# Two transformer blocks on one core: three DVE low halves, one small product, the expert loads and a gather put at other places

## The reference

```python
h = h + g1[:, None, :] * ((ga * y_ret + gb * y_dsa) @ w_o[l])
u2 = modulate(rmsnorm(h, norm_ffn_g[l]), sh2, sc2)
h = h + g2[:, None, :] * hier_moe(u2, ...)
...
gl = (t @ w_gr + b_gr)                  # 4 groups: each token takes its best group
gsel = jnp.argmax(gl, axis=-1)
el_sel = ...                            # the 4 experts of that group
vals, ids = lax.top_k(el_sel, 2)        # two experts of it, with softmax weights
hid = silu(x @ w1[e]) * (x @ w3[e]) * gate
y = sum over e of hid @ w2[e]
```

## Time and profile before

| what | value |
|---|---|
| median of 3 runs | 750.55 us (749.89 to 751.17) |
| the profiled execution | 748.99 us |
| its span, first to last instruction | 747.7 us |
| PE busy | 713.5 us (95%) |
| DVE busy | 500.1 us (67%) |
| ACT busy | 379.3 us (51%) |
| POOL busy | 90.6 us (12%) |
| HBM read | 162.33 MB, mean 219 GB/s |
| mean granted TensorE clock | 0.998 |

### The profile page before, as it was taken

One profiled execution on the slowest core, in us unless ns is written; L12 is line 12 of the kernel. 1 busy time (PEld: TensorE's weight loads), 2 busy tenths in 40 slices (PEclk: granted clock), 3 DMA queues, 4 the chain that ended last, 5 costly groups with the idle time before them and its releaser, 6 DMA issues.

```text
span 747.7 us, 9899 instructions
## 1 busy us (share of the span) xinstructions
PE 713.5 (95%) x3766; PEld 573.2 (77%) x3766; DVE 500.1 (67%) x738; ACT 379.3 (51%) x549; POOL 90.6 (12%) x71
## 2 busy tenths in 40 slices
PE   3899999999999989899999999989999999999997
PEld 0587766778788867788887777769888877788886
DVE  1464784345578773765577898887998675565854
ACT  1354423556445333743557786757634538644532
POOL 0252484330010000000000000011001500000000
PEclk9999999999999999999999999999999999999999
DMA  9999886757336940656678999964444575545541
GB/s 318 362 289 375 279 322 238 253 201 258 107 138 206 357 140 10 192 197 194 187 231 294 368 355 358 366 231 141 144 139 140 149 222 164 158 127 196 169 140 57
DMA packets 100670, 164.07 MB, mean 219 GB/s; under 512 B 10768, under 2 KB 45293, under 8 KB 100494
## 3 DMA queue, kind: packets, MB, share of 16 engines
q1 hardware_dynamic: 98718, 155.53, 62.6%
q0 software_dynamic: 1904, 7.90, 3.1%
HBM read 162.33 MB, written 1.08 MB: 219 GB/s over the span
## 4 chain that ended last, share of the span: by engine, by line
PE 80%; DVE 9%; ACT 4%; DMA 3%; POOL 2%; SPq 1%; issue 1%; ACTq 0%; DVEq 0%
PE p L573 22%; PE p L575 21%; PE p L574 21%; DVE s_rawr L1843 3%; PE p L642 3%; PE p L631 2%; PE p L1235 2%; ACT s_hi L1396 2%; PE p L701 1%; DMA s_ZC<-in_w_ada_dram 1%; PE p L677 1%; DMA s_raw<-in_w_exp_up_dram 1%; POOL s_BI L491 1%; ACT s_L L1446 1%; PE p L689 1%
## 5 line engine op out<-in xcount | busy, mean ns | idle before, releaser
L1843 DVE TENSOR_TENSOR s_rawr<-s_raw,s_hi 128x1024 fp32r<-128x1024 f32 x223 | 271.3, 1248 | 50.2 <-ACT s_hi L1396 49.9
L1396 ACT ACTIVATE s_hi<-s_raw 128x1024 fp32r<-128x1024 f32 x240 | 244.5, 1053 | 83.8 <-PE p L575 52.7
L573 PE MATMUL p<-s_hi,s_Ah 128*128 128x512 f32 (+1 forms) x464 | 186.7, 402 | 2.4 <-POOL s_rawr L472 1.0
L575 PE MATMUL p<-s_hi,s_Al 128*128 128x512 f32 (+1 forms) x464 | 179.7, 387 | 0.0
L574 PE MATMUL p<-s_rawr,s_Ah 128*128 128x512 f32 (+1 forms) x464 | 179.3, 387 | 0.0
L573 PEld LDWEIGHTS p<-s_hi,s_Ah 128*128 128x128 f32 x464 | 87.2, 188 | 29.1 <-issue 8.0
L575 PEld LDWEIGHTS p<-s_hi,s_Al 128*128 128x128 f32 x464 | 87.2, 188 | 18.5
L574 PEld LDWEIGHTS p<-s_rawr,s_Ah 128*128 128x128 f32 x464 | 87.4, 188 | 15.7 <-issue 0.2
L573 PE MATMUL p<-s_hi,s_Bh 128*128 128x512 f32 x192 | 77.1, 402 | 2.6 <-DVE s_rawr L1843 2.6
L575 PE MATMUL p<-s_hi,s_Bl 128*128 128x512 f32 x192 | 75.6, 394 | 0.0
L574 PE MATMUL p<-s_rawr,s_Bh 128*128 128x512 f32 x192 | 75.4, 393 | 0.0
(11 more groups left out here) (375 smaller groups left out, 874.0 us busy)
## 6 DMA issues: line engine op xcount, KB each, us to landing
s_raw<-in_w_in_dram SPq DMA_DIRECT2D x80, 512.0 KB, 4.1
s_GS<-in_w_ada_dram SPq DMA_DIRECT2D x16, 1024.0 KB, 8.1
s_raw<-in_w_exp_gate_dram SPq DMA_DIRECT2D x64, 256.0 KB, 4.1
s_raw<-in_w_exp_up_dram SPq DMA_DIRECT2D x64, 256.0 KB, 4.9
s_raw<-in_w_exp_down_dram SPq DMA_DIRECT2D x32, 512.0 KB, 5.4
s_raw<-in_w_gate_dram SPq DMA_DIRECT2D x16, 512.0 KB, 5.7
s_raw<-in_w_ret_out_dram SPq DMA_DIRECT2D x8, 512.0 KB, 3.5
s_raw<-in_w_o_dram SPq DMA_DIRECT2D x8, 512.0 KB, 8.4
```

The lines of the kernel that those rows point to most:

```text
L573: pe.matmul(o, xh, wh, start=start, stop=False)
L575: return pe.matmul(o, xl, wh, start=False, stop=stop)
L1396: act.activation(T.hi[:, i % NHL, :], T.raw[:, i % NRAW, :], ACT.Copy).then_inc(*S.hi(i))
L1843: dve.tensor_tensor(T.lo[:, i % NRAW, :], T.raw[:, i % NRAW, :], T.hi[:, i % NHL, :].bitcast(F32), ALU.subtract).then_inc(*S.lo_dve(i))
```

## The change

It makes four edits.

1. Around the merged branches. DVE's `branch("ro1", ...)` stands behind one low half (`wo0` piece 2) where it stood behind two; the following low halves move back by one each against the turns' low parts. On PE, `wo0` pieces 0 and 1 go together, the turn M4 comes behind both, and `ada_product(10)` stands between M4 and M6 instead of behind `wo0`. On ACT, `ada_copy(10)` moves to between the roundings of M4 and M6.
2. On SP, the pieces of experts 0 to 3 (as far as `up4`) are queued right behind the first register's load, and each further register is loaded just before the pieces that use it.
3. On PE, `gather_third()` stands right behind the big gather instead of behind `up0`'s second piece.
4. On DVE, `rows_low(0)` moves from the middle of the router's chain to behind P, beside `rows_low(1)`.

```diff
@@ sp_program
     q.wait_ge(*S.dve_route.at("order"))
-    base.extend(sp.value_load(T.gi[0:1, j:j + 1], min_val=0, max_val=12) for j in range(4))
-    pieces(len(PIECES) - done[0])
+    for j in range(4):
+        base.append(sp.value_load(T.gi[0:1, j:j + 1], min_val=0, max_val=12))
+        pieces((AT[f"up{4 * j + 4}", 0] if j < 3 else len(PIECES)) - done[0])
@@ pe_program
-    uses("wo0", 0, 1, A, merged)
+    uses("wo0", 0, 2, A, merged)
     m_cols("M", ("ro0", "ro1"), 4)
-    uses("wo0", 1, 2, A, merged)
+    ada_product(10)
     m_cols("M", ("ro0", "ro1"), 6)
     uses("wo0", 2, 4, A, merged)
...
-    ada_product(10)
     wo1(0, 0, 2)
...
+    gather_third()
     q.wait_ge(*S.act_ple.at("pl", 0, 1))
     q.wait_ge(*S.dve_ada.at(11))
     for h in range(4):
         q.wait_ge(*S.act_gather.at("hi", h))
         q.wait_ge(*S.dve_gather.at("lo", h))
         up_piece(0, h)
-        if h == 1:
-            gather_third()
@@ act_program
     his(1)
+    ada_copy(10)
     cols("M", 6, T.Ah)
     his(2)
...
-    his_to(AT["pl", 0])
-    ada_copy(10)
     his_to(AT["pl", 1])
@@ dve_program
     lows_to(AT["wo0", 2])
     cols("M", 0, T.Ah, T.Al), cols("M", 2, T.Ah, T.Al)
+    lows_to(AT["wo0", 3])
+    branch("ro1", 0, "ga1", 4, True)
     lows_to(AT["wo1", 0])
-    branch("ro1", 0, "ga1", 4, True)
     cols("M", 4, T.Ah, T.Al)
-    lows_to(AT["wo1", 2])
+    lows_to(AT["wo1", 1])
     cols("M", 6, T.Ah, T.Al)
     lows_to(AT["wo1", 3])
...
-    rows_low(0)
     q.wait_ge(*S.dve_route.at("big"))
...
     for tt in range(2):
         dve.tensor_scalar(T.P[:, tt, :], ..., ALU.is_equal).then_inc(*S.dve_route("P", tt))
-    rows_low(1)
+    rows_low(0), rows_low(1)
     ada_end(11)
```

## The result

| | before | with the change |
|---|---|---|
| median | 750.22 us (749.86 to 751.17, 4 runs) | 744.89 us (744.71 to 745.63, 4 runs) |
| the profiled execution, its span | 748.99, 747.7 us | 744.99, 743.7 us |

The ratio is 0.9935, 95% interval [0.9923, 0.9948]: faster by 0.65%. Forecast were 746.0 us, from 744.6 to 748.3.

A forecast was written before the change was run, and what follows sets the result against it. PE was taken as the bound (80% of the span), time being won only where it stops waiting or clocks higher. Terms -2.02 and -2.56 sum to -4.58 us, taking the median from 750.55 to 746.0 us, range 744.6 to 748.3.

The forecast's parts named there:

- The term: Merged branches: PE's waits of 1.21 us at M4 and 0.81 us at M6's low part vanish, -2.02 us.
- given back at x: Rival: the branches' gain is lost at residual x or in ACT's longer list, 748.0 us; chance 0.07.
- The bound by which the router's chain would gain: Router: moving rows_low(0) gains 1.19 us there if "ranks" are done early; kept as the other bound to +1.19.
- The sum: Gather to gates: load order, third gather and rows_low(0) together give -2.56 us, DVE's list being the bound.
- the new wait before the gates: PE, before the gates' matmuls: waits 0.7 us for the route chain, starting them at 325.4 instead of 327.96.
- 0, hidden behind ACT: First expert piece: the earlier load gains 0, since ACT's rounding starts at 312.65 with or without it.
- the 2.38 us are filled, and with them the fall goes: PE between gather and first expert piece: third gather fills the 2.38 us wait, and the clock no longer falls to 0.50.
- Its price: Rival: the clock falls all the same near the gather, costing 1.9 us, 747.9 us; chance 0.12, of it 0.04 break-even.
- the argument against a fall: Third gather, the 1.21 us wait's stretch and waits of 1.1 and about 1 us at 503 and 506 showed none.
- The slower rival: Expert stage: moved register loads do not fit SP's pauses, +8.8 - 4.6, giving 754.8 us; chance 0.04.

The follow-up runs named there:

- run 1: Changed kernel with DVE's rows_low(0) put back in the middle of the router's chain: 744.19 us, ratio 0.9926 to the kernel before.
- run 2: Changed kernel with SP's four registers loaded together again before the first expert load: 745.28 us, ratio 0.9945 to the kernel before.
- run 12: Kernel before, with only gather_third() moved right behind the big gather: 750.35 us, one execution.
- run 5: Changed kernel with SP's registers loaded together first and rows_low(0) back in the router's chain: 749.6 us, one execution.
- run 10: Second measurement of run 1's kernel, on one chip with the changed kernel: 744.44 us, ratio 0.9932.
- run 3: Changed kernel with gather_third() put back behind up0's second piece: 748.05 us, ratio 0.9972 to the kernel before.
- run 11: Kernel before, with only SP's register loads spread among the expert pieces: 749.37 us, one execution.
- run 6: Changed kernel with only DVE's order around the merged branches undone, PE and ACT keeping the new order: 744.65 us, one execution.
- run 4: Changed kernel with all reordering around the merged branches undone: 747.62 us, ratio 0.9974 to the kernel before.
- run 8: Changed kernel with rows_low(0) back in the router's chain and the gates' matmuls behind up0's fourth piece: 744.21 us, ratio 0.992 to the kernel before.

## Why the prediction was right, and where it was not

**Edit 1: mechanism right, -2.69 for -2.02.** M4's and M6's low parts end 7.40 and 9.84 us behind M; worked out were 270.8 and 273.3, that is 7.46 and 9.96. The term was mis-sized in what a wait costs: I took the idle times of the rows, 1.21 + 0.81. What goes with a wait is also the tail by which its last matmul outlasts the step (0.16, which I had worked out for the first wait and then not counted). From start to start the two waits cost 1.37 and 0.97 us, 2.34 in all. `wo1` begins 13.80 us behind M, against 16.32 before, a gain of 2.52, 0.18 beyond the waits. The last 0.17 lie in the twelve matmuls of `wo1`'s first piece: from its start to the next group of matmuls it takes 2.90 us before and 2.73 with the change, and from there to "ranks" the two traces keep step. Both have one pattern. In this stretch a piece right behind another takes 2.72 or 2.73 us from start to start, and one right behind a turn, the product or a wait 2.85 to 2.93. With the change, two more of `wo0`'s pieces and `wo1`'s first stand right behind a piece. At `wo0` that saves 0.35, of which 0.17 go into the two turns (0.94 us in place of 0.77). Nothing was given back at x: it is ready 15.41 us behind M instead of 15.98, and PE shows no wait behind it, so that rival is out.

**Edit 4: right, +1.21 for +1.19.** The free place became 1.00 us of idle DVE, the gather waits for the second row part, and run 1 takes the term away alone. The bound by which the router's chain would gain did not hold in any run.

**Edits 2 to 4 between gather and gates.** The sum came out; one step in it, the landing of the load, did not (next paragraph). The parts (-3.75 there, with +1.19 ahead of it) came as -3.67 and +1.21, -2.46 together for -2.56. The first piece was ready at 313.36 (low half from 312.13, 1.23 long) and PE came at 314.86, 1.5 us of slack where 1.35 was forecast; the new wait before the gates was 0.46 instead of 0.7, which with PE's restart (the gates' row is 1.51 us long, where it was 1.41 without a wait) is nearly a match.

**Edit 2: right beside edit 4 only.** "0, hidden behind ACT" holds (run 2). Of "the first load from 308.77 to 307.1 and its landing from 311.8 to 310.15" the first half held: the issue came 1.64 us nearer to "ranks". The landing came 0.06 nearer, since the transfer took 4.6 us. It cost nothing, because ACT was not there before 9.90 us behind "ranks" and the load landed at 8.98. The cover was edit 4's own delay of 1.2 us, and the sentence that priced edit 2 did say that `big_high(0)` was moved by edit 4; what it did not say was that edits 2 and 4 hide the same lateness twice. Without edit 4, ACT comes to its place 8.7 us behind "ranks", and what edit 2 is worth varies with the landings. Gather to gates is 17.00 and 17.71 us without it (runs 12 and 5), 16.34 and 16.61 with it (runs 1 and 10), so 0.4 to 1.4 us, and whatever the clock does behind it. The changed kernel pays for both: with edit 2 in place, edit 4 is a plain loss, and by the steps the kernel of runs 1 and 10 is the better one.

**The clock.** That it would not fall near 315 us was right. Its price was right too: 1.9 us were taken from the earlier trace rows; runs 3 and 11 give 1.65, and the difference is the restart behind the wait and the tail ahead of the gather, which are there without a fall too. But "the 2.38 us are filled, and with them the fall goes" read one cause from one case: a wait of 2.01 us at the same place left the clock alone (run 11) and one of 2.02 did not (run 3, which had an earlier wait as well). One row was misread in the argument against a fall: near 506 us the kernel before has idle times of 0.18 and 0.22 us, not "about 1 us"; the 1.11 at 503.17 is there. The Trainium skill ("TensorE: Matmul & The Clock Gate", Part 1) says that the slow clock is the default and activity releases it. The traces agree in that each fall recorded ahead of the last 10 us begins during a wait of PE or within 1 us behind it; that sentence does not say which wait is followed by one, and between 1.1 and 2.4 us of idling these runs show both outcomes.

**The slower rival** is out: gates to end, which holds the three moved register loads, is 419.90 us before and 419.97 with the change, and 419.78 with edit 2 undone. The three loads took 0.54 us each, at 356.87, 405.61 and 441.02 us.

**The sum.** -5.08 for -4.58, of which the profile showed 4.0 for a reason outside the change: the 264 us ahead of M. The median is 1.1 us below the forecast of 746.0: 0.5 lie in the steps behind M, 0.3 in the median before, which was 750.55 in the forecast and 750.22 in the result, and the remaining 0.3 no row places.

## What to carry to other kernels

Add what a wait costs from the starts of the rows around it, the tail and the restart included, not from the idle time alone. Where two edits remove the same lateness, price each of them with and without the other: of edits 2 and 4 only one was needed, and the one that costs nothing on the critical path was the one to keep. And measure such edits by distances between events of one trace: the medians, which hold a start that varies by up to 2.9 us, show 1.2 us only dimly.

## What the runs showed of the hardware

**The two falls behind a wait at the gates lasted twice as long as the two behind the wait at the first piece.** In runs 5 and 12 a wait of 1.83 and 1.14 us was followed by the gates (12 matmuls of 16 columns) and then by about 7 us at half the clock (325.2 to 332.2 and 327.0 to 334.0 us; the windows above hold stretches at full clock too), at a cost of 3.5 and 3.3 us against the mean of 419.7. In the kernel before and in run 3 the fall lasted 3.6 us. Whether the small matmuls do this is not shown: near 26 us falls of both lengths are recorded (7.0 us in runs 1 and 5, 3.6 in others) with the same instructions behind the wait. The length of the idle time alone does not decide either. In all fourteen profiles a wait of 1.42 us at 122 to 126 us had no fall behind it, nor had the 1.2 us waits before M4 (4 profiles), nor 0.46 to 0.72 us at the gates; the 1.2 us wait before the gather had none in six of seven profiles, and in run 3 one only behind the next wait.

**The start varies, and the column of the granted clock does not always show it.** At about 26 us PE waits for the first low part, in every profile. Rows before, then with edit 2 alone, PE and window:

```profile
26.44 0.36 PE L573 MATMUL p<-s_Ah,s_hi 128*128 128x256 f32 x1 [2.21 <-DVE s_Al L1862]
26.63 0.28 PE L574 MATMUL p<-s_Al,s_hi 128*128 128x256 f32 x1
26.75 0.28 PE L575 MATMUL p<-s_Ah,s_rawr 128*128 128x256 f32 x1
```

```profile
28.00:32.00 4.00, 4.00 (x34) 2.43 (x34) 3.09 (x3) 1.04 (x2) 1.00 (x1) 1.00 1.05 388
```

```profile
26.66 0.55 PE L574 MATMUL p<-s_Ah,s_hi 128*128 128x256 f32 x1 [2.15 <-DVE s_Al L1863]
27.00 0.41 PE L575 MATMUL p<-s_Al,s_hi 128*128 128x256 f32 x1
27.22 0.41 PE L576 MATMUL p<-s_Ah,s_rawr 128*128 128x256 f32 x1
```

```profile
28.00:32.00 4.00, 4.00 (x20) 3.82 (x18) 2.54 (x2) 1.25 (x2) 1.20 (x1) 1.00 1.05 387
```

The steps are 0.12 us in the first and 0.21 in the second, 34 matmuls in four microseconds against 20, and the granted clock reads 1.00 in both. The same wait of 2.1 to 2.2 us thus stands ahead of full steps in three profiles (before, and runs 2 and 6, with M at 263.2 to 263.4) and of half-speed steps, for 2.8 to 4.7 us, in the changed kernel's first profile and runs 3, 4, 8 and 11; in the other six profiles the wait was 3.5 to 4.3 us, and the steps slowed there too, at once or a little later. In all eleven of these M lies at 264.2 to 266.1. From the end of the wait to M pass 236.9 to 237.2 us in the three profiles and 237.9 to 239.5 in the eleven, so the slow stretch moves M; what decides whether it comes, nothing here shows.
